# RWKV layer: readout weights and first two tiles loaded in the recurrence, keys and b as one stationary operand

## The reference, cut to what matters

```
def step(s, inp):
    r_t, lw_t, k_t, v_t, a_t, b_t = inp
    sa = jnp.einsum('dbhij,dbhj->dbhi', s, a_t)
    s = s * jnp.exp(lw_t)[..., None, :] + sa[..., None] * b_t[..., None, :] + v_t[..., None] * k_t[..., None, :]
    return s, jnp.einsum('dbhij,dbhj->dbhi', s, r_t)
...
yf = y[0] + jnp.flip(y[1], 1)
mean = jnp.mean(yf, axis=-1, keepdims=True)
var = jnp.mean(jnp.square(yf - mean), axis=-1, keepdims=True)
yn = ((yf - mean) * lax.rsqrt(var + GN_EPS)).reshape(B, T, D).astype(gate.dtype) * lnx_g + lnx_b
bonus = jnp.sum(r[None] * k_dir * r_k, axis=(0, -1))[..., None] * v
o = (yn + bonus.reshape(B, T, D)) * jax.nn.silu(gate)
return o @ w_out
```

## Time and profile before

| | |
|---|---|
| median of 3 runs | 2908.8 us (2900.32 to 2911.53) |
| profiled execution, its own time | 2916.49 us |
| span of the profile | 2914.8 us |
| mean granted TensorE clock | 0.924 of full |
| PE busy | 2473.9 us (85%) |
| DVE, ACT, POOL busy | 1355.7, 706.0, 458.6 us |

### The profile page before, as it was taken

One profiled execution on the slowest core, in us unless ns is written; L12 is line 12 of the kernel. 1 busy time (PEld: TensorE's weight loads), 2 busy tenths in 40 slices (PEclk: granted clock), 3 DMA queues, 4 the chain that ended last, 5 costly groups with the idle time before them and its releaser, 6 DMA issues. The chain is left out here.

```text
span 2914.8 us, 48605 instructions
## 1 busy us (share of the span) xinstructions
PE 2473.9 (85%) x19670; PEld 1453.8 (50%) x19670; DVE 1355.7 (47%) x2690; ACT 706.0 (24%) x1271; POOL 458.6 (16%) x426
## 2 busy tenths in 40 slices
PE   5998855988899999987179999978998399989988
PEld 2553435944444444433145566457777146455553
DVE  1651556523511111111888895956665571044442
ACT  3110440012111111111325541133333113044441
POOL 0000142300111111111000000032221220034550
PEclk8999777996999999999599999999999799999999
DMA  7111510016499999995615555254442932021001
GB/s 267 38 58 39 194 22 18 6 58 223 177 372 392 391 416 409 395 382 214 254 41 157 156 141 179 112 148 124 128 133 72 362 118 96 6 40 21 13 30 65
DMA packets 328930, 471.43 MB, mean 162 GB/s; under 512 B 151465, under 2 KB 225107, under 8 KB 304005
## 3 DMA queue, kind: packets, MB, share of 16 engines
q1 hardware_dynamic: 302645, 373.92, 37.1%
q10 hardware_dynamic: 12960, 69.21, 5.9%
q0 software_dynamic: 13104, 25.19, 2.3%
HBM read 413.82 MB, written 76.55 MB: 168 GB/s over the span
## 5 line engine op out<-in xcount | busy, mean ns | idle before, releaser
L1956 PE MATMUL psum<-ex_w,hT 128*64 128x512 f32 (+1 forms) x1104 | 326.7, 611 | 28.3 <-DMA ex_w<-in_exp_w_up 26.6
L1956 PEld LDWEIGHTS psum<-ex_w,hT 128*64 128x64 f32 (+1 forms) x1104 | 124.5, 157 | 224.5 <-issue 222.5
L4022 POOL TENSOR_SCALAR mla_pool<-mla_pool,at_stats 128x768 f32<-128x768 f32 x64 | 140.2, 2203 | 254.7 <-DVE at_stats L4040 254.7
L2189 DVE COPY slot_act_t<-psum 128x256 f32<-128x256 f32 x45 | 19.1, 425 | 325.1 <-PE psum L1964 325.1
L551 PE MATMUL psum<-hT,weights 128*128 128x512 f32 x384 | 166.8, 592 | 0.0
L1972 PE MATMUL psum<-ex_w,slot_act_t 128*64 128x512 f32 (+1 forms) x552 | 163.4, 597 | 1.4 <-DVE slot_act_t L2189 1.4
L1941 POOL DMA_INDIRECT scratch_ys<-slot_out,slot_row x45 | 45.3, 1006 | 464.9 <-issue 401.5
L551 PEld LDWEIGHTS psum<-hT,weights 128*128 128x128 f32 x384 | 73.0, 190 | 86.7 <-issue 86.1
L2145 ACT ACTIVATE slot_silu<-psum 128x256 f32<-128x256 f32 x45 | 17.3, 384 | 397.2 <-PE psum L1956 397.2
L3192 PE MATMUL psum<-rs_r_ident,rs_b 64*32 64x96 f32 x1536 | 85.6, 249 | 16.6 <-POOL rs_k_ident L3164 12.8
L3920 PE MATMUL psum<-mla_kT,at_qT 128*128 128x512 f32 (+1 forms) x256 | 93.3, 489 | 2.6 <-DVE at_qT L4032 1.6
(11 more groups left out here) (597 smaller groups left out, 4863.6 us busy)
## 6 DMA issues: line engine op xcount, KB each, us to landing
ex_w<-in_exp_w_gate SPq DMA_DIRECT2D x64, 1024.0 KB, 9.2
ex_w<-in_exp_w_up SPq DMA_DIRECT2D x64, 1024.0 KB, 18.8
ex_w<-in_exp_w_down ACTq DMA_DIRECT2D x60, 1024.0 KB, 10.3
mod_ring<-in_w_mod SPq DMA_DIRECT2D x12, 2048.0 KB, 13.4
scratch_features<-tokens SPq DMA_DIRECT2D x96, 256.0 KB, 3.7
weights<-in_w_in SPq DMA_DIRECT2D x6, 2048.0 KB, 8.1
ex_w<-in_mod_w SPq DMA_DIRECT2D x6, 2048.0 KB, 13.1
ex_w<-scratch_ys SPq DMA_DIRECT2D x8, 1536.0 KB, 19.0
```

Of the source, the lines that this page charges most:

```text
L1956: mm = pe.matmul(bank[at:at + n, :], XT[:, k, at:at + n], W[:, 0:2, k * DE:(k + 1) * DE], start=(k == 0), stop=(k == KD - 1))
L4022: pool.tensor_scalar(Pm[:, q % 2, u, :], Pm[:, q % 2, u, :], st[:, 3, u:u + 1], None, ALU.mult)\
```

## The change

A class `Readout` is made before the recurrence and used in both stages. It owns buffers that the recurrence uses and the readout takes over: the two operands RI and KI, the inverse TB, and the four feature buffers. `w_out` is loaded in three pieces into RI, KI and TB, tile 1's rows into the feature buffers, g and b into RI and AM; tile 0 has buffers of its own.

In the recurrence SP loads tile 0 at unit 8, and parameters, tile 1 and `w_out` once the last carry and GpSimd's last copies are done. GpSimd does its part of tiles 0 and 1 there; VectorE does the norm of tile 0 and mean and centring of tile 1 between and after the state updates of the last unit; ScalarE squares and roots tile 0. The last state update, whose result nothing reads, is left out. The readout begins with turning tile 0, without the loads that are done. SP no longer waits for the stores at the stage's end; the wait stands in the readout ahead of tile 2.

In `prepare`, keys and b lie side by side in KI, so that one matmul with 64 stationary columns takes the place of two with 32. GpSimd copies b there too (two copies more for each half), and SP loads b and A behind those copies of the unit before.

```
+    def load_params(self, sp):
+        sp.dma_start(self.b, self.I["rwkv_lnx_b_2"][0].partition_broadcast(P)).then_inc(self.S["params_in"], 16)
+        sp.dma_start(self.g, self.I["rwkv_lnx_g_2"][0].partition_broadcast(P)).then_inc(self.S["params_in"], 16)
+
+    def load_weights(self, sp):
+        src = self.I["rwkv_w_out_2"][0].rearrange("(k p) n -> p k n", p=P)
+        for at, w in self.w:
+            sp.dma_start(w, src[:, at:at + w.shape[1], :]).then_inc(self.S["w_in"], 16)
+
+    def mean(self, dve, step, j):
+        s = j % 2
+        yj = self.y[s]
+        dve.wait_ge(self.in_y[s], 32 * (j // 2 + 1))
+        step(dve.tensor_tensor(yj, yj, self.y2[s], ALU.add))
+        step(dve.tensor_reduce(self.st[:, s, 0, :], self.heads(yj), AX.X, ALU.add))
+        step(dve.tensor_scalar(self.st[:, s, 0, :], self.st[:, s, 0, :], 1.0 / HD, None, ALU.mult))
...
+    def finish(self, dve, step, j):
+        s = j % 2
+        yj = self.y[s]
+        dve.wait_ge(self.S["rms_done"], j + 1)
+        step(dve.reciprocal(self.st[:, s, 3, :], self.st[:, s, 2, :]))
+        step(dve.tensor_tensor(self.heads(yj), self.heads(yj), self.wide(self.st[:, s, 3, :]), ALU.mult))
+        dve.wait_ge(self.S["params_in"], 32)
+        step(dve.tensor_tensor(yj, yj, self.g, ALU.mult))
+        dve.wait_ge(self.S["shifted"], j + 1)
+        step(dve.tensor_tensor(yj, yj, self.bon[s], ALU.add))
+        dve.wait_ge(self.in_bg[s], 32 * (j // 2 + 1))
+        dve.tensor_tensor(yj, yj, self.gate[s], ALU.mult).then_inc(self.S["normed"], 1)
...
                 if u:
 
+                    sp.wait_ge(spread_[half], 7 * u)
                     sp.wait_ge(S["a_mm"], g - 4)
...
-                if u:
-
-                    sp.wait_ge(spread_[half], 5 * u)
...
+                if u == 8:
+                    for b in range(2):
+                        sp.wait_ge(y_st[b], 16 * 4 * 2 * JC)
+                    R.load(sp, 0)
             store(N - 2, CH - 1)
+            sp.wait_ge(S["w_mm"], 8 * N)
+            for half in range(2):
+                sp.wait_ge(spread_[half], 7 * N)
+            R.load_params(sp)
+            R.load(sp, 1)
+            R.load_weights(sp)
             store(N - 1, CH // 2 - 1)
             store(N - 1, CH - 1)
-            for b in range(2):
-                sp.wait_ge(y_st[b], 16 * 4 * N)
...
-                    pool.tensor_copy(KI[E_, ks, :, HD:W], KT[E_, ks, :, :]).then_inc(spread_[half], 1)
-                    pool.wait_ge(spread_[half], 5 * u + 2)
-                    pool.tensor_copy(KI[O_, ks, :, 0:RC], KT[O_, ks, :, :]).then_inc(spread_[half], 1)
-                    pool.wait_ge(spread_[half], 5 * u + 3)
+                    for p, part in enumerate((E_, O_)):
+                        pool.tensor_copy(KI[part, ks, :, k_at[p]], KT[part, ks, :, :]).then_inc(spread_[half], 1)
+                        pool.wait_ge(spread_[half], 7 * u + 2 + p)
+                    pool.wait_ge(b_in[half], 32 * (u + 1))
+                    for p, part in enumerate((E_, O_)):
+                        pool.tensor_copy(KI[part, ks, :, b_at[p]], BT[part, ks, :, :]).then_inc(spread_[half], 1)
+                        pool.wait_ge(spread_[half], 7 * u + 4 + p)
...
+            for j in range(2):
+                R.values(pool, j)
...
                 for ch in range(CH):
-                    for sides, lhs in ((sside, (BT[E_, k, ch, :], BT[O_, k, ch, :])),
-                                       (vside, (KI[E_, k, ch, HD:W], KI[O_, k, ch, 0:RC]))):
-                        for p, part in enumerate((E_, O_)):
-                            m = pe.matmul(K.bank[scb(u, k)[p]][sides[p], ch * P:ch * P + W], lhs[p], RI[part, k, ch, :],
-                                          start=True, stop=True)
+                    for p, part in enumerate((E_, O_)):
+                        m = pe.matmul(K.bank[scb(u, k)[p]][kb_at[p], ch * P:ch * P + W], KI[part, k, ch, kb_at[p]],
+                                      RI[part, k, ch, :], start=True, stop=True)
                 m.then_inc(S["sc_mm"], 1)
                 pe.wait_ge(S["a_out"], 2 * g)
                 for ch in range(CH):
                     for p, part in enumerate((E_, O_)):
-                        m = pe.matmul(K.bank[AB[p]][ch * RC:(ch + 1) * RC, 0:W], AT[part, k, ch, :], KI[part, k, ch, :],
+                        m = pe.matmul(K.bank[AB[p]][ch * RC:(ch + 1) * RC, 0:W], AT[part, k, ch, :], KI[part, k, ch, ki_at[p]],
                                       start=True, stop=True)
                 m.then_inc(S["a_mm"], 1)
...
+                        if (u, q) != (N - 1, CH - 1):
+                            state(u, q)
...
+            step = Chain(dve, S["early"])
+            R.mean(dve, step, 0)
+            state(N - 1, 0)
+            R.centre(dve, 0)
+            state(N - 1, 1)
+            R.sum(dve, 0)
+            state(N - 1, 2)
+            R.finish(dve, step, 0)
+            R.mean(dve, step, 1)
+            R.centre(dve, 1)
...
+                    if u == N - 1 and q == 1:
+                        R.square(act, 0)
                     if u >= 0 and q == 2:
                         read(u, 0)
+                    if u == N - 1 and q == 2:
+                        R.root(act, 0)
...
-            load(0)
-            sp.dma_start(g[:, :], I["rwkv_lnx_g_2"][0].partition_broadcast(P)).then_inc(S["params_in"], 16)
-            sp.dma_start(b[:, :], I["rwkv_lnx_b_2"][0].partition_broadcast(P)).then_inc(S["params_in"], 16)
-            load(1)
-            sp.dma_start(wb[:, :, :], I["rwkv_w_out_2"][0].rearrange("(k p) n -> p k n", p=P)).then_inc(S["w_in"], 16)
             M.load(sp, 0)
...
+            for b in range(2):
+                sp.wait_ge(S[f"y_st{b}"], 16 * 4 * 2 * NT)
             for j in range(2, NT):
-                load(j)
+                sp.wait_ge(S["turned"], j - 1)
+                R.load(sp, j)
...
-            norm(0)
+            R.square(act, 1)
             copy_in(0)
-            norm(1)
+            R.root(act, 1)
...
-            norm(0)
+            R.sum(dve, 1)
             copy_in(0)
-            norm(1)
+            R.finish(dve, step, 1)
```

More of the change, by code:

```diff
@@ L3036, in _, with __init__, weights, load @@
                 leave(i + 1)
-def rwkv_scan(K, I, rw, Y, fm, lane_out, Dg):
+class Readout:
+    SEMS = ("y_st0 y_st1 in_y0 in_y1 in_bg0 in_bg1 params_in w_in x_in centred sq_done summed rms_done normed scaled "
+            "shifted")
+    def __init__(self, K, I, S, sb, rw, Y, bonus):
+        self.K, self.I, self.S, self.rw, self.Y, self.bonus = K, I, S, rw, Y, bonus
+        CH, CT = P // RC, KD
+        self.RI, self.KI = sb("rs_r_ident", [P, CT, CH, RC + HD]), sb("rs_k_ident", [P, CT, CH, P])
+        self.TB, self.AM = sb("rs_inverse", [P, H2, P]), sb("rs_am", [P, H2, P])
+        self.in_scan = [sb("rs_" + n, [P, CT, CH, RC]) for n in "abkr"]
+        self.yb = sb("rs_y", [P, 2, 512])
+        self.st = sb("ro_stats", [P, 2, 4, H2])
+        first = [sb("ro_" + n, [P, D]) for n in ("y", "y2", "bonus", "gate")]
+        second = [t[:, :, :, :].rearrange("p k c t -> p (k c t)") for t in self.in_scan]
+        self.y, self.y2, self.bon, self.gate = ([a[:, :], b] for a, b in zip(first, second))
+        ri, ki = (t[:, :, :, :].rearrange("p k c t -> p (k c t)") for t in (self.RI, self.KI))
+        tb, am = (t[:, :, :].rearrange("p h t -> p (h t)") for t in (self.TB, self.AM))
+        self.g, self.b, self.sums = ri[:, 2 * D:3 * D], am[:, 0:D], am[:, D:2 * D].rearrange("p (a n) -> p a n", a=2)
+        rows = lambda t, n: t[:, 0:n * D].rearrange("p (k n) -> p k n", n=D)
+        self.w = [(0, rows(ri, 2)), (2, rows(ki, 4)), (6, rows(tb, 2))]
+        self.in_y, self.in_bg = (S["in_y0"], S["in_y1"]), (S["in_bg0"], S["in_bg1"])
+        self.heads = lambda ap: ap.rearrange("p (h n) -> p h n", n=HD)
+        self.wide = lambda ap: ap.unsqueeze(2).broadcast_to([P, H2, HD])
+    def weights(self, k, n):
+        at, w = [e for e in self.w if e[0] <= k][-1]
+        return w[:, k - at, n]
+    def load(self, sp, j):
+        s, rows = j % 2, slice(j * P, (j + 1) * P)
+        sp.dma_start(self.y[s], self.Y[0, rows, :]).then_inc(self.in_y[s], 16)
+        sp.dma_start(self.y2[s], self.Y[1, rows, :]).then_inc(self.in_y[s], 16)
+        sp.dma_start(self.bon[s], self.rw[V_, rows, :]).then_inc(self.in_bg[s], 16)
+        sp.dma_start(self.gate[s], self.rw[GATE_, rows, :]).then_inc(self.in_bg[s], 16)
+    def load_params(self, sp):
[5 more added lines that the diff above has]
+            sp.dma_start(w, src[:, at:at + w.shape[1], :]).then_inc(self.S["w_in"], 16)
+    def values(self, pool, j):
+        pool.wait_ge(self.S["params_in"], 32)
+        pool.wait_ge(self.in_bg[j % 2], 32 * (j // 2 + 1))
+        v = self.bon[j % 2]
+        by_head = v.rearrange("p (k h n) -> p k h n", k=KD, n=HD)
+        pool.tensor_tensor(by_head, by_head, self.bonus[:, :, j, :].unsqueeze(3).broadcast_to([P, KD, 2, HD]), ALU.mult)\
+            .then_inc(self.S["scaled"], 1)
```

(32 more changed lines are left out.)

120 lines of the change are left out of this document (40 added, 80 removed).

## The result

The changed kernel takes 2876.2 us (median of 4 runs, 2870.7 to 2883.8), against 2904.6 for the kernel before, measured beside it: a ratio of 0.9903 (95% interval 0.9878 to 0.9928), 28 us less. The profiled execution after has a span of 2882.0, 32.8 less than the one before (2914.8).

A forecast was written before the change was run, and what follows sets the result against it. It took TensorE to bound the recurrence, and transfers and the norm behind them the readout's first 71 us. +9.9 - 2.4 + 1.3 - 22.1 = -13.3 us gave 2895.5 us, range 2881 to 2909.

The forecast's parts named there:

- Edge between scores and A: In each preparation on TensorE, the new shape change from scores to A costs 0.15 us more: +9.9 us.
- Fewer instructions: In the eleven slots, 16% fewer matmuls cut TensorE's 15.3 us of issue stalls by 16%: -2.4 us, bounds 0 and -4.
- rival without an edge: In the preparations, A slips in among the scores and the shape change costs nothing: 2885.6 us in total, chance 0.25.
- GpSimd's copies: At the start, TensorE waits for GpSimd's two more copies for each half: +1.3 us once, later free.
- Readout: Early loads and norm bring tile 2's turn 24.5 us sooner after a stage start 2.4 later: -22.1 us.
- blocked tail: Rival: in the last slot, GpSimd's values slow four VectorE norm operations, 8 us: 2903.5 us in total, chance 0.14.
- Tile 0's early transfers: Tile 0's four transfers at unit 8 of the recurrence cost nothing, as SP waits there anyway.
- score step that gets slower: Rival: wider tiles' weight loads aren't hidden, 0.05 us more for each score step: +13, 2922 us, chance 0.09.

## Why the prediction was right or wrong, step by step

**Edge between scores and A (+9.9): right.** The preparation went from 0.960 to 1.133 us, 0.173 more where 0.15 was forecast, and the eight score steps stayed. Over 77 preparations in sight that is 13.3 us; the first carry behind the output group absorbed 2.0 (eleven times 0.857 to 0.675 us): about +11. The run with the token carry shows the edge by itself: there A is followed by its own shape, and the next group starts 0.19 us after A instead of 0.33:

```profile
2190.99 0.40 PE L3306 MATMUL psum<-rs_k_ident,rs_a 64*32 64x96 f32 x16
2191.18 0.22 PE L3316 MATMUL psum<-rs_inverse,rs_am 64*32 64x32 f32 x2
```

That is 0.14 more at the change of shape, the price read from the earlier trace rows (the small carry also goes to tiles that A has already left, as A did among the scores before). The Trainium skill's rule that changing the tiling mode drains TensorE (TensorEngine Tiling (Array Packing), Key Properties) agrees with this.

**Fewer instructions (-2.4, bounds 0 and -4): this step failed.** The idle time fell by 19.0 us (21.6 to 2.6). Measured by the lengths of the stretches between groups, against their medians, the stalls cost 31 us before and 5 after: about -26. (About 1 of these 5 is no stall but the first group and preparation at the lower clock, see below.) I had let the stalls shrink with the count of instructions, 16% for 16%, without asking what they were. They stand where a packet of instructions comes later than the stream can do without it, so a step of 17% in pace (3.97 to 4.78 us for each packet) took nearly all of them. The bounds should have been 0 and the whole of the issue rows at the least. Edge and stalls together, +11 - 26 = -15, are the slots' -14.7; the forecast had +7.5. That alone is 22 us, more than the whole miss of the profiled execution. It is also why the total came out below the rival without an edge (2885.6), though the edge is there.

**GpSimd's copies (+1.3): right.** From the stage's first instruction to the first score it was 10.2 us instead of 8.9 (9.8 to 10.2 in other kernels with these copies). The stretch from there to the first slot took 21.6 us instead of 19.1; that is not the copies, as kernels with the same lines took 18.7 to 21.6 there. Behind a wait of 1.8 us for ScalarE TensorE ran from 1937.0 at a granted clock of 0.50, the lower level (1.2 GHz), past the first slot's start at 1943.7.

**Readout (-22.1): right,** with each sight of it: start of the stage +2.0 against the last slot (forecast 2.4), tile 0 turned at once, tile 2 late. The blocked tail showed as one operation of 2.9 us instead of 1.2 beside GpSimd, 1.7 us instead of the rival's 8. But the reason lay in the loads alone: the early norm by itself cost 7 us.

**Tile 0's early transfers (nothing): too low, but little.** The prediction counted SP's time and 2 MB on engines at 0.46, and no delay for anything else on these engines. In the changed kernel's trace a stall of 1.6 us lies within them, 1.0 to 2.3 us in the kernels like it.

**The sum** of the profiled execution: 2.9 (the stage began later, before anything changed) + 3.8 (start to first slot) - 14.7 - 22.2 - 2.5 (after the turn of tile 2, not looked into) = -32.7, against 32.8 measured. The score step that gets slower was a wrong rival: the steps kept their 0.083 us.

**Open:** how a data transfer holds up a packet of instructions, and how much of the stalls would go if the loads of the next unit were spread or moved. No run did that.

## What to carry to other kernels

A stall with no releaser is a term of its own: look for its cause (here each ended just behind a packet of instructions, mostly one that came late while data transfers filled the DMA engines), and until it is known, bound its change by the whole of it, as a small step in pace can take all. Small matmuls in dense groups pay for their instructions, so merging two of the same stream can win even where it adds an edge between shapes. And work moved ahead of a stage boundary is free only if its engine isn't the last to cross: what the next stage waits for first (bytes in a queue) must start early, and the arithmetic that isn't late may stay behind.

## What the runs showed of the hardware

Instructions of TensorE cost idle time from some 4.4 us per packet of 16 KB downwards (8 to 12 stalls in eleven slots at 4.3 to 4.4 us, 26 or 27 at 4.0, at most 6 from 4.6 on), with this stage's loads beside them: before the change the packets ahead of a stall started 5.05 us behind the one before, the others 3.85, at 0.79 and 0.39 of the DMA engines busy. A wait that is already satisfied isn't free on TensorE: 2816 pairs of them lengthened the slots by 153 us, 0.054 us each, while one pair behind each score matmul, with 0.08 us of stream to hide in, left the median preparation at 1.134. And a 128x128 carry of four passes hardly depends on its columns: 0.64 us at 128, 0.56 at 32.
